# One of the first layer's twelve modulation slabs taken from the chain behind the output projection and computed in the neighbourhood attention

## The reference

```python
m = silu(cvec) @ w_mod[l] + b_mod[l]          # 2 vectors, 1024 -> 6 * 1024: six shifts, scales, gates
h = rmsnorm(x) * (1 + m[1]) + m[0]
z = h @ w_in[l]                               # q, k, v of three mixers, and the gates
a, b, c = diff_attention, neighbourhood_attention, bidirectional_retention
x = x + m[2] * (sum(sigmoid(gates) * [a w_pa, b w_pb, c w_pc]) @ w_out[l])
h = rmsnorm(x) * (1 + m[4]) + m[3]
x = x + m[5] * expert_choice_ffn(h)           # 16 experts of 1024 x 1024, three matrices each
```

## Time and profile before

| what | value |
|---|---|
| median of 3 runs | 2008.8 us (2007.84 to 2009.1) |
| profiled execution, its own time | 2007.38 us |
| its span in the profile | 2005.6 us |
| TensorE busy | 1862.2 us, 93% |
| bytes moved by DMA | 552.40 MB, 275 GB/s over the span |
| first layer's experts | 564.48 us to about 1003 us |
| second layer's experts | 1547.77 us to about 1989 us |

### The profile page before, as it was taken

One profiled execution on the slowest core, in us unless ns is written; L12 is line 12 of the kernel. 1 busy time (PEld: TensorE's weight loads), 2 busy tenths in 40 slices (PEclk: granted clock), 3 DMA queues, 4 the chain that ended last, 5 costly groups with the idle time before them and its releaser, 6 DMA issues.

```text
span 2005.6 us, 19735 instructions
## 1 busy us (share of the span) xinstructions
PE 1862.2 (93%) x8266; PEld 937.4 (47%) x8266; DVE 600.5 (30%) x1156; ACT 340.3 (17%) x787; POOL 66.4 (3%) x55
## 2 busy tenths in 40 slices
PE   7999999999999988888799999999999998888887
PEld 3565556555544333233355555565555333333323
DVE  1432356455211101101034333655543102011112
ACT  3232331000211001000132233210003010101102
POOL 0200000000200000000002000000001000000000
PEclk9999999999999999999999999999999999999999
DMA  9422281442399999999982222616325999999996
GB/s 390 188 74 82 81 346 43 172 164 108 142 428 429 429 429 428 428 429 430 426 325 95 84 90 91 256 42 251 126 94 218 430 428 430 429 429 428 429 430 268
DMA packets 53545, 552.40 MB, mean 275 GB/s; under 512 B 5840, under 2 KB 10832, under 8 KB 12240
## 3 DMA queue, kind: packets, MB, share of 16 engines
q1 hardware_dynamic: 49680, 548.51, 65.7%
q10 hardware_dynamic: 3776, 2.62, 0.4%
HBM read 546.91 MB, written 4.19 MB: 275 GB/s over the span
## 4 chain that ended last, share of the span: by engine, by line
PE 66%; DMA 30%; DVE 2%; ACT 1%; issue 1%; SPq 0%; POOL 0%; POOLq 0%; DVEq 0%; ACTq 0%
PE psum L970 12%; PE psum L1161 12%; DMA ring<-in_w_up 12%; DMA ring<-in_w_down 12%; PE psum L828 12%; PE psum L1054 6%; PE psum L830 6%; PE psum L1076 4%; DMA wide<-in_w_gate 3%; PE psum L410 2%; DMA ring<-in_w_gate 2%; PE psum L889 1%; DMA ring<-in_w_in 1%; PE psum L1141 1%; PE psum L810 1%; PE psum L791 1%
## 5 line engine op out<-in xcount | busy, mean ns | idle before, releaser
L970 PE MATMUL psum<-hT,ring 128*128 128x384 f32 x768 | 255.7, 486 | 0.0
L828 PE MATMUL psum<-hT,ring 128*128 128x384 f32 x720 | 240.5, 488 | 0.0
L1161 PE MATMUL psum<-dense 128*64 128x512 f32 x864 | 195.3, 596 | 31.7 <-DMA dense<-in_w_up 17.5
L1161 PE MATMUL psum<-ring,dense 128*64 128x512 f32 x832 | 189.9, 600 | 25.9 <-DMA ring<-in_w_gate 14.9
L970 PEld LDWEIGHTS psum<-hT,ring 128*128 128x128 f32 x768 | 145.6, 190 | 100.9
L828 PEld LDWEIGHTS psum<-hT,ring 128*128 128x128 f32 x720 | 134.5, 190 | 87.0 <-issue 1.4
L1161 PEld LDWEIGHTS psum<-dense 128*64 128x64 f32 x864 | 62.4, 137 | 154.4 <-issue 130.0
L1891 DVE TENSOR_TENSOR state<-state,psum 128x512 f32<-128x512 f32 x32 | 22.0, 688 | 373.2 <-PE psum L1161 335.2
L1054 PE MATMUL psum<-dense,ring 128*128 128x384 f32 x384 | 131.9, 487 | 0.0
L830 PE MATMUL psum<-ring,hT 128*128 128x512 f32 x288 | 126.5, 592 | 0.0
L1161 PEld LDWEIGHTS psum<-ring,dense 128*64 128x64 f32 x832 | 60.2, 137 | 140.8 <-issue 120.2
(11 more groups left out here) (225 smaller groups left out, 1692.6 us busy)
## 6 DMA issues: line engine op xcount, KB each, us to landing
ring<-in_w_up SPq DMA_DIRECT2D x32, 2048.0 KB, 38.0
ring<-in_w_in SPq DMA_DIRECT2D x60, 1024.0 KB, 11.3
dense<-in_w_up SPq DMA_DIRECT2D x30, 2048.0 KB, 40.1
ring<-in_w_down SPq DMA_DIRECT2D x30, 2048.0 KB, 40.1
dense<-in_w_gate SPq DMA_DIRECT2D x24, 2048.0 KB, 36.5
wide<-in_w_down SPq DMA_DIRECT2D x20, 2048.0 KB, 40.2
ring<-in_w_gate SPq DMA_DIRECT2D x20, 2048.0 KB, 37.6
wide<-in_w_gate SPq DMA_DIRECT2D x20, 2048.0 KB, 38.5
```

The source lines that it names most:

```text
L828: last = M.matmul(psum[:, bank, 0:T], ring[:, n % RING, k, cols], hT[:, k, :], start=k == 0, stop=k == KD - 1)
L970: last = M.matmul(psum[:, Z[1], 0:T], ring[:, n_gate % RING, k, (j % 4) * P:(j % 4 + 1) * P], hT[:, k, :], start=k == 0, stop=k == KD - 1)
L1161: last = M.matmul(psum[HALF * half:HALF * (half + 1), bank, :], lhsT(k), w[:, kk, half * SLAB:(half + 1) * SLAB], start=k == 0, stop=k == ...
```

## The change

Slab 10 of layer 0's modulation joins the dense list, whose slabs go through the ring and are computed in the neighbourhood attention; the chain of layer 0 then has two slabs, both of layer 1. Where the dense list needs more steps than there are, the first two steps are merged. The filler up to which the first gate product waits is now named as the first of the layer's chain.

```diff
-        DENSE_MODS = [[4, 5, 6, 7, 8, 9, 11], [4, 5, 6, 7, 8, 9]]
-        CHAIN = [[(0, 10), (1, 0), (1, 2)], [(1, 10), (1, 11)]]
+        DENSE_MODS = [[4, 5, 6, 7, 8, 9, 10, 11], [4, 5, 6, 7, 8, 9]]
+        CHAIN = [[(1, 0), (1, 2)], [(1, 10), (1, 11)]]
...
             for n in range(1, len(m)):
                 steps.append([("modT", l, m[n - 1])] + ([("mod", l, m[n + 1])] if n + 1 < len(m) else [("modT", l, m[n])]))
+            if len(steps) > A_STEPS - 7:
+                steps = [steps[0] + steps[1]] + steps[2:]
             return [[]] * (A_STEPS - 7 - len(steps)) + steps
...
-        DENSE_FILLERS = [f_of("mod", l, 10) for l in range(DEPTH)]
+        DENSE_FILLERS = [f_of(*CHAIN_FILL[l][0]) for l in range(DEPTH)]
```

## The result

The changed kernel takes 2014.95 us (median of 8 runs, 2013.07 to 2016.28), the kernel before 2008.41 (8 runs): ratio 1.003, interval 1.002 to 1.004. That is +6.5 us where +4.9 was forecast, inside the range and slower, as forecast.

A forecast was written before the change was run, and what follows sets the result against it. TensorE was taken to bound the kernel up to the routing, back-to-back DMA loads the first layer's experts. Terms 0 + 2.6 + 2.3 = +4.9 us on 2008.8 gave 2013.7 us, range 2010.6 to 2016.2.

The forecast's parts named there:

- Part 1: Layer 0's routing and experts: the shorter chain starts experts sooner but the load stream ends them; 0 us, bounds -2.4 to 0.
- The rival of the shorter stream: Layer 0's expert loads: buffer 5's early release lets one more load ahead, stream 4.9 us shorter, 2008.8 us; chance 0.11 (with kept routing).
- Part 2: Layer 0's attention, step 7: one more product and transposition, paid in full; +2.6 us, bounds 0 to 3.6.
- Part 3: Boundary to layer 1: slabs move one ring position, so the first waits for the very last expert load; +2.3 us, bounds 0 to 4.7.

## Why the prediction was right, and where it was short

- **Part 1, the shorter chain: 0 forecast, 0 measured** (457.8 against 458.0 us). The order of issue was the reason: with buffer 5 first, 3.1 us appear. The rival of the shorter stream named that condition rightly, and it didn't hold in the change.
- **Part 2, the attention: 2.6 forecast, 2.74 in the trace, 2.4 by the run with the places undone.** The work in step 7 is paid in full. That the idle of later steps would have taken it is shown only in part: the idle went, most of the gain didn't come.
- **Part 3, the ring places: 2.3 forecast.** The mechanism is shown from both sides, undone (-4.1) and alone (+1.9 where the clock is taken to have stayed). The product started 7.5 us after the issue of its slab, as taken from w_pb, and the wait measured 2.2; in the five other traces with a late slab it is 7.4 to 7.9 us. The form that the prediction quotes from the Trainium skill (DMA: Bandwidth & Descriptors, Anatomy of one DMA) is one fitted for DMAs that GpSimd issues, and these are SyncE's: it was right not to add it up.
- **The mis-sized term** is part 3's sum: it moved the work behind the product in full but kept the product at 1.92 us. After 2.11 us of idle TensorE's clock fell to half in this trace, 1.7 us that no term held and no rival named. The trace of the kernel before could have told it: of its waits for loads in the experts the two longest, 1.99 us at 789.73 and 2.38 us at 1780.46, are both followed by 16 matmuls that take 5.35 us instead of 3.65. The forecast put a wait of 2.3 us at a place where nothing absorbs such a fall. The changed kernel's two fastest runs took 2013.1 us, 4.7 above the kernel before and near the 4.9 forecast; the six others took 2014.5 to 2016.3. That the clock stayed up in those two is likely but not shown, as neither has a trace.
- **The rest.** 1.0 of the profiled 7.5 us is the start's own scatter. By medians the 6.5 us are 2.4 for the attention and 4.1 for the ring places; of the latter the trace gives 2.2 to the wait and 1.7 to the clock.

## What to carry to other kernels

Where slabs rotate through a ring, one slab more shifts all that follow: look at which buffer the next stage's first loads inherit, and at what stands behind them in the queue. A load taken out of a stretch where the DMA has room is worth nothing to the saturated stretch behind it, unless the order of issue lets another load take its room; then ask what fills next (here all buffers, until the first consumer starts). Work put into a gap gains only if the gap stands behind it on the same chain, and the slabs that follow aren't freed later by it. And a mean clock of 1.00 over hundreds of us doesn't say that the clock held: look for a group of matmuls that takes longer than its like, and ask what stands behind TensorE at the place where the change puts a new wait.

## What the runs showed that was not expected

The granted clock fell to about half behind an idle time of 2.05 or 2.11 us at the layers' boundary in two traces and stayed at 1.00 behind 2.44, 2.36 and 2.16 us in three others. Four of the five are traces of one and the same program, the kernel before with its places shifted, and one of these four fell.

The same goes for the waits in the experts. With those five counted, TensorE, once it has started, stands idle for 1.9 us or more 28 times in the twelve traces of this case. Behind 16 of these times the clock falls to half, behind 12 it stays; the first are 1.99 to 2.70 us long, the others 1.97 to 2.67, so their length doesn't tell which it will be. No fall came without such an idle time, but for the tail of a run, where TensorE has no more work.

What a fall costs depends on where it comes. In the experts it costs nothing that can be told, though the matmuls take up to 1.7 us longer: the kernel before and the one with its places shifted have the same program from the first expert product to the end of layer 0's last one, and this takes 438.8, 438.4 and 438.4 us in the three traces with a fall there and 438.6 and 438.7 in the two without. The loads set the time, and the next idle times shrink. At the boundary nothing stands behind TensorE that could absorb it: from the last down product to the first z product it is 13.7 us without a late slab, 15.9 to 16.2 with one (+2.2 to 2.5), and 17.5 or 17.6 with one and a fall (+3.8 or 3.9).

So a run's mean clock doesn't say where the time went. It counts the falls that cost nothing, and the tail: the changed kernel's profiled run has 0.996 with three falls, of which one cost time, and the kernel before 0.998 with two that cost none.
